# The up projections of a second SwiGLU FFN by one level of Strassen's scheme, fp32r matmuls of 256 columns

## The reference

```python
def swiglu(h, w1, w3, w2):
    return (jax.nn.silu(h @ w1) * (h @ w3)) @ w2
h = modulate(rms_norm(x, ffn2_norm[l]), sh3, sc3)
x = x + 0.5 * g3[:, None, :] * swiglu(h, ffn2_w1[l], ffn2_w3[l], ffn2_w2[l])
```

## Time and profile before

| | us |
|---|---|
| median of 3 runs | 1123.32 |
| the runs | 1123.31, 1124.42, 1123.32 |
| span of the profiled execution | 1122.3 |
| mean granted clock of TensorE in it | 0.981 |
| second FFN, up projections (PE) | 745.3 to 987.3 |
| second FFN, down projection (PE) | 987.3 to about 1110 |

### The profile page before, as it was taken

How to read it: one execution, slowest core, us unless ns; L and a number is a source line. 1 busy time by engine, 2 the same in 40 slices (tenths; PEclk the granted TensorE clock), 3 DMA queues, 4 the chain that set the end, 5 groups by cost and what they waited for, 6 DMA issues and landing times.

```text
span 1122.3 us, 13691 instructions
## 1 busy us (share of the span) xinstructions
PE 1066.8 (95%) x4902; PEld 873.7 (78%) x4902; DVE 606.9 (54%) x700; ACT 404.6 (36%) x516; POOL 163.9 (15%) x149
## 2 busy tenths in 40 slices
PE   3899999999999999998998888999999999999997
PEld 3788888888888888786776767778888888888885
DVE  5877677633342326659899899553333333322324
ACT  3242222222311223575865665343232222222211
POOL 2211111000000101016382533010000000000100
PEclk9799999999999999998999899999999999999999
DMA  8678788622222223221111111213322223222222
GB/s 300 230 246 278 262 264 262 203 91 97 94 94 93 94 94 139 78 82 49 56 57 57 51 43 39 76 57 108 98 93 93 93 95 105 98 94 94 93 94 75
DMA packets 37393, 132.41 MB, mean 118 GB/s; under 512 B 4080, under 2 KB 4336, under 8 KB 37232
## 3 DMA queue, kind: packets, MB, share of 16 engines
q1 hardware_dynamic: 28992, 100.83, 26.7%
q0 software_dynamic: 8368, 31.13, 8.2%
HBM read 129.85 MB, written 2.10 MB: 118 GB/s over the span
## 4 chain that ended last, share of the span: by engine, by line
PE 83%; DVE 10%; issue 3%; DMA 2%; ACT 2%; SPq 0%; DVEq 0%; ACTq 0%
PE psum L1127 25%; PE psum L1129 24%; PE psum L1128 24%; PE psum L1362 2%; PE psum L1376 1%; DVE qk L976 1%; DMA ada<-wada 1%; PE psum L1332 1%; DVE qk L975 1%; PE psum L1164 1%; DVE acc L697 1%; DMA raw<-wu 1%; DVE wlo L673 1%; PE psum L1233 1%; PE psum L1303 1%
## 5 line engine op out<-in xcount | busy, mean ns | idle before, releaser
L673 DVE TENSOR_TENSOR wlo<-raw,whi 128x1024 fp32r<-128x1024 f32 x166 | 209.3, 1261 | 340.9 <-ACT whi L358 340.7
L358 ACT ACTIVATE whi<-raw 128x1024 fp32r<-128x1024 f32 x168 | 177.9, 1059 | 563.6 <-PE psum L1129 549.0
L1127 PE MATMUL psum<-hhi,whi 128*128 128x512 f32 x896 | 359.6, 401 | 10.5 <-DVE sg L927 5.4
L1128 PE MATMUL psum<-hlo,whi 128*128 128x512 f32 x896 | 351.9, 393 | 0.0
L1129 PE MATMUL psum<-hhi,wlo 128*128 128x512 f32 x896 | 351.6, 392 | 0.0
L1127 PEld LDWEIGHTS psum<-hhi,whi 128*128 128x128 f32 x896 | 170.3, 190 | 50.9 <-DVE wlo L673 7.7
L1129 PEld LDWEIGHTS psum<-hhi,wlo 128*128 128x128 f32 x896 | 170.1, 190 | 36.3
L1128 PEld LDWEIGHTS psum<-hlo,whi 128*128 128x128 f32 x896 | 170.4, 190 | 35.4 <-issue 1.9
L1127 PE MATMUL psum<-ghi,whi 128*128 (+1 forms) x352 | 138.5, 394 | 0.0
L1129 PE MATMUL psum<-ghi,wlo 128*128 (+1 forms) x352 | 138.1, 392 | 0.0
L1128 PE MATMUL psum<-glo,whi 128*128 (+1 forms) x352 | 136.8, 389 | 0.0
(11 more groups left out here) (172 smaller groups left out, 970.7 us busy)
## 6 DMA issues: line engine op xcount, KB each, us to landing
raw<-wu SPq DMA_DIRECT2D x168, 512.0 KB, 3.3
ada<-wada POOLq DMA_DIRECT2D x56, 512.0 KB, 5.0
ada<-wada SPq DMA_DIRECT2D x16, 512.0 KB, 4.7
x<-xt SPq DMA_DIRECT2D x2, 1024.0 KB, 10.2
out<-outt SPq DMA_DIRECT2D x8, 256.0 KB, 2.2
bd<-bd POOLq DMA_DIRECT2D x1, 1024.0 KB, 5.1
dif<-consts POOLq DMA_DIRECT2D x1, 448.0 KB, 6.1
resets<-consts POOLq DMA_DIRECT2D x1, 256.0 KB, 6.9
```

The source lines that it names most:

```text
L358: nc.scalar.activation(whi[:, slot, :], raw[:, slot, :], ACT.Copy).then_inc(hi_done, 1)
L673: nc.vector.tensor_tensor(wlo[:, slot, :], raw[:, slot, :], whi[:, slot, :], ALU.subtract).then_inc(lo_done, 1)
L1127: nc.tensor.matmul(dst, a, rhi, start=start, stop=False)
L1128: nc.tensor.matmul(dst, a, rlo, start=False, stop=False)
```

## The change

The product of the weights (two FF blocks x eight k blocks) and the activations (512 tokens) is seen as 2 x 2 blocks: FF block, half of the k blocks, half of the tokens. One level of Strassen's scheme (in a form that shares sums) gives its four result blocks from seven products of 128 x 512 by 512 x 256, each four k blocks long, of sums of the operands' quarters. This is done for w1 and w3 of the second FFN, 11 pairs of FF blocks, 22 groups. Each product is still split in three fp32r matmuls per k block, now with 256 columns.

Weights: a new input `ws` holds four quarters of 128 x 512 per group. SP loads two of them twice and one once, POOL adds the fourth twice with an accumulating DMA into two places of the first four (`add_fourth`), and makes two more sums (`long_sums`). ACT and DVE split the seven operands in four parts per group (`group_upper`, `group_lower`). Two groups are in flight; the second set of buffers lies in the memory of `raw`, the upper and lower parts of four of the operands in that of `whi` and `wlo`, one set only.

Activations: `forms` (DVE), `forms_upper` (ACT) and three `token_sum` (POOL) make seven upper and seven lower operands once, ahead of the stage. The first product follows k by k, the second waits for the tenth lower part, the fourth for the twelfth.

Results: `first_copy`, `middle_sums`, `last_sums` combine the products; silu and gating run on two FF blocks at a time, and the gated result is kept in float32 (`g2`). Its upper and lower parts are made later, from the last group on and during the first half of the down projection. Nine more of the unread matmuls are issued by PE ahead of the stage. The first FFN is unchanged.

```diff
--- before.py
+++ after.py
+U_DOWN2 = U_OUT + 8
+N_UNITS = U_DOWN2 + KF
...
+B21, NT3, T1, NT4, T2, B12, B11 = range(PRODUCTS)
+DOWN_AT = (U_FFN1 + 2 * KF, U_DOWN2)
...
+        def sum_bank(i, s):
+            b, half = ((3 * s, 0), (3 * s + 1, 0), (3 * s + 1, 1), (3 * s + 2, 0), (7, s), (3 * s + 2, 1), (3 * s, 0))[i]
+            return bank[b][:, HALF_T * half:HALF_T * half + HALF_T]
...
+            def load_group(j, s):
+                for i in range(2):
+                    sp_.dma_start(sraw_a[s][:, 2 * i:2 * i + 2, :], twice(quarter(j, s, i))).then_inc(base_loaded[s], 16)
+                sp_.dma_start(sraw_b[s][:], quarter(j, s, 2)).then_inc(base_loaded[s], 16)
...
+            sp_.wait_ge(scored, STEPS * HEADS)
+            load_group(0, 0)
+            sp_.wait_ge(lo_done, U_DOWN2)
+            load_group(0, 1)
+            with sp_.Fori(1, PAIRS) as j:
+                for s in range(2):
+                    sp_.wait_ge(slo_done, 8 * j + (4 * s - 4))
+                    load_group(j, s)
+            sp_.wait_ge(slo_done, 4 * GROUPS)
+            for u in (U_DOWN2, U_DOWN2 + 1):
+                sp_.dma_start(raw[:, u % 2, :], wu[u]).then_inc(raw_loaded[u % 2], 16)
+            with sp_.Fori(U_DOWN2 // 2 + 1, N_UNITS // 2) as j:
+                unit_pair(j)
...
+            def add_fourth(j, s):
+                pool.wait_ge(base_loaded[s], 48 * j + 48)
+                pool.dma_start(sraw_a[s][:, 1:3, :], twice(quarter(j, s, 3)), accum_op=ALU.add
+                               ).then_inc(sum_loaded[s], 16)
+            def long_sums(j, s):
+                if not (isinstance(j, int) and j == 0 and s == 0):
+                    pool.wait_ge(slo_done, 8 * j + (4 * s - 1))
+                pool.wait_ge(base_loaded[s], 48 * j + 48)
+                pool.wait_ge(sum_loaded[s], 16 * j + 16)
+                nc.gpsimd.tensor_tensor(xs[:, 0, :], sraw_a[s][:, 2, :], sraw_a[s][:, 0, :], ALU.add).then_inc(xs_done, 1)
+                pool.wait_ge(xs_done, 4 * j + (2 * s + 1))
+                nc.gpsimd.tensor_tensor(xs[:, 1, :], xs[:, 0, :], sraw_b[s][:], ALU.add).then_inc(xs_done, 1)
+            def token_sum(i, a, b, op):
+                nc.gpsimd.tensor_tensor(form(t32, i), a, b, op).then_inc(t32_done, 1)
+            add_fourth(0, 0)
+            long_sums(0, 0)
+            add_squares(2, 0)
+            add_squares(2, 1)
+            add_fourth(0, 1)
+            pool.wait_ge(h32_done, 4)
+            token_sum(0, h_right[:, 4:8, :], h_left[:, 4:8, :], ALU.subtract)
+            pool.wait_ge(h32_done, 8)
+            pool.wait_ge(t32_done, 1)
+            token_sum(1, h_right[:, 0:4, :], form(t32, 0), ALU.subtract)
+            pool.wait_ge(t32_done, 2)
+            token_sum(2, h_left[:, 0:4, :], form(t32, 1), ALU.subtract)
+            with pool.Fori(0, PAIRS - 1) as j:
+                long_sums(j, 1)
+                add_fourth(j + 1, 0)
+                long_sums(j + 1, 0)
+                add_fourth(j + 1, 1)
+            long_sums(PAIRS - 1, 1)
...
+            def group_upper(j, s, part):
+                if isinstance(j, int) and j == 0 and s == 0:
+                    if part < 2:
+                        act.wait_ge(unit_used, U_DOWN2 - 1 + part)
+                else:
+                    act.wait_ge(prod_done, 14 * j + (7 * s - (5, 3, 1, 0)[part]))
+                if part != 2:
+                    act.wait_ge(base_loaded[s], 48 * j + 48)
+                if part < 2:
+                    act.wait_ge(sum_loaded[s], 16 * j + 16)
+                    src, dst = sraw_a[s][:, 2 * part:2 * part + 2, :], hi4[:, 2 * part:2 * part + 2, :]
+                elif part == 2:
+                    act.wait_ge(xs_done, 4 * j + (2 * s + 2))
+                    src, dst = xs[:], hix[:, 0:2, :]
+                else:
+                    src, dst = sraw_b[s][:], hix[:, 2, :]
+                nc.scalar.activation(dst, src, ACT.Copy).then_inc(shi_done, 1)
+            def first_copy(j, s):
+                act.wait_ge(prod_done, 14 * j + (7 * s + 1))
+                if not (isinstance(j, int) and j == 0):
+                    act.wait_ge(evac_done, 8 * j + (4 * s - 7))
+                nc.scalar.activation(p1c[:, s, :], sum_bank(0, s), ACT.Copy).then_inc(p1_copied, 1)
...
+            def forms_upper():
+                for i in range(KD):
+                    d = ORDER[i]
+                    act.wait_ge(htmp_done, 2 * KD + i + 1)
+                    nc.scalar.activation(plain_form(fhi, i), token_halves(tmp[:, i % 2, :], i), ACT.Identity,
+                                         bias=mod("sh3", d)).then_inc(fhi_done, 1)
+                    nc.scalar.activation(h32[:, d, :], tmp[:, i % 2, :], ACT.Identity,
+                                         bias=mod("sh3", d)).then_inc(h32_done, 1)
+                for i, (f, t) in enumerate(((T1, 0), (NT3, 3), (T2, 1), (NT4, 2))):
+                    if f == NT3:
+                        act.wait_ge(nt3_done, 1)
+                    else:
+                        act.wait_ge(t32_done, t + 1)
+                    nc.scalar.activation(fhi[:, f, :], t32[:, t, :], ACT.Copy).then_inc(fhi_done, 1)
+            def group_phase(j, s, last=False):
+                first_copy(j, s)
+                if last:
+                    act.wait_ge(prod_done, PRODUCTS * (GROUPS - 1) + 2)
+                    hi_u(U_DOWN2)
+                    g2_upper(0)
+                    act.wait_ge(prod_done, PRODUCTS * (GROUPS - 1) + 4)
+                    hi_u(U_DOWN2 + 1)
+                    g2_upper(1)
+                    g2_upper(2)
+                    return
+                for part in range(4):
+                    group_upper(j + s, 1 - s, part)
+                if s == 0:
+                    group_silu(j)
...
+            for part in range(1, 4):
+                group_upper(0, 0, part)
+            nc.scalar.preload_act_table(ACT.Silu)
+            forms_upper()
+            ffn_up_pairs()
...
+            def group_lower(j, s, part):
+                dve.wait_ge(shi_done, 8 * j + (4 * s + part + 1))
+                if part < 2:
+                    src, up, dst = (t[:, 2 * part:2 * part + 2, :] for t in (sraw_a[s], hi4, lo4))
+                elif part == 2:
+                    src, up, dst = xs[:], hix[:, 0:2, :], lox[:, 0:2, :]
+                else:
+                    src, up, dst = sraw_b[s][:], hix[:, 2, :], lox[:, 2, :]
+                nc.vector.tensor_tensor(dst, src, up, ALU.subtract).then_inc(slo_done, 1)
+            def middle_sums(j, s):
+                dve.wait_ge(prod_done, 14 * j + (7 * s + 5))
+                dve.wait_ge(p1_copied, 2 * j + (s + 1))
+                if not (isinstance(j, int) and j == 0 and s == 0):
+                    dve.wait_ge(evac_done, 8 * j + 4 * s)
+                nc.vector.tensor_tensor(u2[:], sum_bank(4, s), p1c[:, s, :], ALU.subtract).then_inc(evac_done, 1)
+                dve.wait_ge(evac_done, 8 * j + (4 * s + 1))
+                nc.vector.tensor_tensor(u34[:], three_banks(s)[:, 0:2, :],
+                                        u2[:].unsqueeze(1).broadcast_to([P, 2, HALF_T]), ALU.add).then_inc(evac_done, 1)
+            def last_sums(j, s):
+                dve.wait_ge(prod_done, 14 * j + (7 * s + 6))
+                dve.wait_ge(evac_done, 8 * j + (4 * s + 2))
+                if s:
+                    dve.wait_ge(silu2_done, 2 * j + 2)
+                elif not (isinstance(j, int) and j == 0):
+                    dve.wait_ge(g2_done, 2 * j)
+                nc.vector.tensor_tensor(csum[:, T:2 * T].rearrange("p (h t) -> p h t", h=2)[:, ::-1, :],
+                                        three_banks(s)[:, 1:3, :],
+                                        u34[:, 0:1, :].broadcast_to([P, 2, HALF_T]), ALU.add).then_inc(evac_done, 1)
+                nc.vector.tensor_tensor(csum[:, HALF_T:T], sum_bank(5, s), u34[:, 1, :], ALU.subtract
+                                        ).then_inc(evac_done, 1)
...
+            def forms():
+                dve.wait_ge(rb_done, 3)
+                dve.wait_ge(cols_ready, 5)
+                for i in range(KD + 1):
+                    if i < KD:
+                        d = ORDER[i]
+                        if i >= 2:
+                            dve.wait_ge(h32_done, i - 1)
+                        nc.vector.scalar_tensor_tensor(tmp[:, i % 2, :], x[:, d, :], scale[:, 2 * KD + d:2 * KD + d + 1],
+                                                       rb(2), ALU.mult, ALU.mult).then_inc(htmp_done, 1)
+                    if i:
+                        dve.wait_ge(fhi_done, i)
+                        dve.wait_ge(h32_done, i)
+                        nc.vector.tensor_tensor(plain_form(flo, i - 1), token_halves(h32[:, ORDER[i - 1], :], i - 1),
+                                                plain_form(fhi, i - 1), ALU.subtract).then_inc(flo_done, 1)
+                nc.vector.tensor_tensor(form(t32, 3), h_right[:, 4:8, :], h_right[:, 0:4, :], ALU.subtract
```

(69 more changed lines are left out.)

217 lines of the change are left out of this document (167 added, 50 removed).

## The result

The changed kernel takes 1150.25 us (median of 4 runs, 1148.44 to 1151.55) against 1123.87 us of the kernel before on the same chip: ratio 1.0227, 95% interval 1.0210 to 1.0244. It is slower by 26 us; forecast were 1114.2 us, with a full range of 1105 to 1136. The profiled execution has a span of 1146.6 us (before 1122.3), 24.3 us more.

The account below looks back on a forecast made before the run. PE alone was taken to bound the stage: 764.8 + 1813 x 0.116 + 3.1 = 978.2 us against 987.3, -9.1 us (matmuls -29.1, start +16.8, end +3.1), giving 1114.2 us; full range 1105 to 1136.

Parts of the forecast that it names:

- The pitch: New stage, start-to-start time of 256-column matmuls: taken as 116 ns, between 112 and 120; one nanosecond is 1.8 us.
- goes with the columns: Reading of the 13.3 ns on top of each 512-column matmul as proportional to columns: 113.3 ns at 256 columns.
- fixed: Rival: the 13.3 ns are a fixed cost per matmul, 120.0 ns at 256 columns, -1.9 us, 1121.4 us; chance 0.17.
- ACT: after the root it converts ...: Stage start: ACT converts 1024, 1024 and 512 wide and loads a table, from 740.7 to 744.8 us, against 743.64 before.
- POOL's three sums: Stage start: three sums of 2.48 us each on POOL; with later ACT and DVE work, last operand at 764.3, about when wanted.
- The 35 first matmuls: Stage start: 12 of the first product and 23 at half clock, done by 764.8 us, leaving 1813 matmuls.
- The hole: Stage start: PE idles from 750.4 to 759.8 us before the second product, then half clock until 764.8.
- Sum ... = 18.75 us. It fits under 19.5: Steady state: the chain refilling a weight buffer takes 18.75 us, within two phases of 19.5, so it costs nothing.
- rival (c): Steady state: accumulating DMA's chain becomes the bound from 5.7 us landing; at 7.4 us, +16 us, 1130 us; chance 0.25.
- Cost 3.1 us: Stage end: down units load only after the last lower part, 12.8 us into a phase of 9.74; PE waits 3.1 us.
- What would show it: List of trace signs: matmul spacing, start hole with half clock, waits between phases, DMA landing time, 3 us end hole.

Follow-up runs that it names:

- the plain fourth: Changed kernel with the fourth quarter's DMA overwriting instead of accumulating (result wrong for the second FFN): 1135.14 us, span 1133.3.

## Why the prediction was wrong

**The pitch was right, by luck.** 116 was taken and 116.2 measured where nothing waits; but it is the mean over 48 matmuls at 113.3 and 36 at 120.0, the two values that I had derived from "goes with the columns" and "fixed" and held for alternatives. "Fixed" holds at distance 0 (120.0, 173.3 and 226.7). 113.3 came at distance 192, where 512 columns take 228.9, so that it equals half of 226.7 is chance. What neither reading has in it is how the operands lie to each other, and that was mine to choose: with the sums' weights moved, all go at 113.3.

**An instruction that I did not follow past its queue.** The largest single wait is in no term of the sum: "ACT: after the root it converts ...", "POOL's three sums" count what is added for the new stage, not who stands behind it. POOL's DMA and two sums were put ahead of the norm's squares, whose chain sets the root. Price 8.8 us (11.8 less the 3.0 from further ahead), and undoing it gave 8.7.

**"POOL's three sums (2.48 each ...)", laid beside DVE at no cost.** They do not lie beside it: 2.2 + 2.2 + 2.1 = 6.5 us of DVE in the stretch that feeds PE. The 35 first matmuls, which I saw done 23.1 us behind the root, were done 28.3 us behind it, and 0.9 more was waited at the fourth product: 6.1 us. The hole was forecast at 9.4 us and the half clock at 5; measured 12.8 and 5. The 0.9 is of the same kind: two lower parts of 1.2 us took 4.5 beside POOL's weight sums.

**"Sum ... = 18.75 us. It fits under 19.5".** The mechanism is rival (c), whose threshold of 5.7 us for the accumulating DMA was hit exactly (5.7, and 6.0 in the chain shown). But at 5.7 my terms give 19.45 us, no stall yet; 21.6 were measured, because more terms were short. The base loads to the last landing took 6.5 and not 6.0; the wlo of 1.25 took 2.31, held by POOL's sum of the same group; and the last lower part waits for DVE's u, csum and lox in their order. Price 9.7 us over 21 phases, 7.2 of it waits and 2.5 the slower pitch behind them, which no term has.

**"Cost 3.1 us" for the end**, measured 4.9, and behind it half clock for 5 us, which I had counted for the hole at the start but not for this one: 1.8 us, and 3.0 in the down stage.

These are 8.8 + 6.1 + 9.7 + 1.8 + 3.0 = 29.4 us, and 3.0 came in from ahead of 707 us: 32.4 of the 33.4 by which the span (1146.6) missed the forecast (1113.2). Of the 3.0, 2.1 are the start of the program (first root at 36.8 instead of 34.8), which varied by as much between executions. The first FFN, from its root to the next, took the same 392.9 us: its up stage was 1.3 us longer, at 229.0 ns instead of 226.7, as the new layout moved whi against the moving tiles, and the stretch ahead of it as much shorter. The remaining 1.0 came in the mixer (166.9 us instead of 165.9 to its first root), whose matmuls of 512 columns use the same places; it was not isolated. The last 1.0 of the 33.4 is not placed.

**"What would show it"** ended with the right rule: matmuls at 0.116 and a time above 1121 mean a wait costed at nothing. There were three: POOL's queue ahead of the norm, POOL beside DVE at the start, and the reload chain with the end behind it. All three were repaired without touching the scheme. As the pitch was right, these are the steps that failed: the chain under 19.5 us, the sums at no cost, and a wait that stood in no term.

## What to carry to other kernels

Where a change adds work to an engine that was idle, list what that engine already has to deliver, in queue order, and put the new work behind it; "idle 85% of the span" says nothing of the microsecond in which it is wanted. A buffer that is refilled by a chain should be handed back in the pieces in which it is read, not when its last reader is done. A short wait can cost more than itself: most runs of narrow matmuls that began behind one kept the slower of two pitches. When a matmul's pitch is not its columns over the clock, move the operands by 64 bytes against each other before counting on it, and look at every stage that shares the buffers.

## What the runs showed of the hardware

- A DVE operation with two inputs in SBUF, begun just after a POOL sum, is held until that ends: 0.42 us became 2.61. POOL's sums are held in turn: 1.27 us became 2.13.
- An accumulating DMA of 512 KB from POOL landed in 5.7 to 5.9 us and took 1.20 us to issue; the same transfer without accumulation 3.9 to 4.0 and 0.72.
- The pitch of fp32r matmuls depends on the distance of weights and moving tile modulo 256 bytes: at 256 columns 113.3 to 120.0 ns, worst at 0; at 512 columns 226.7 to 233.3, best at 0. In the kernels the distances of 64 and 192 gave 113.3 or 117.8 ns at 256 columns, the latter in 24 of 29 phases that began behind a wait of PE (at 192) and in a whole stage (at 64).
- Behind idle times of PE of 1.9 (with the plain fourth), 3.9, 4.8, 5.5 and 12.8 us the granted clock was half for 3 to 6 us; behind another of 1.9 us (with the sums' weights moved by 64 bytes) and several of 1.3 to 1.7 it stayed full. Where unread matmuls filled 9 and 4 us of the two holes at the start, PE came back at full clock from both.
